# A ninth gate tile in the scan's block, early loads of the first experts, and a last stage by column halves

## What is computed

```python
z = h @ p['w_in']                      # its last 3*1024 columns are the three branch gates zg
# three mixers on parts of z: RWKV-7 time mixing (both directions), 2-D attention, S5 state space
gates = jax.nn.sigmoid(zg).reshape(..., 3, D_MODEL)
merged = jnp.sum(jnp.einsum('btnc,ncd->btnd', y, p['w_branch']) * gates, axis=2)
x = layer_norm(alpha * x + gate1 * (merged @ p['w_out']))
h = x * (1 + scale2) + shift2
# router: the 8 best of 64 experts for each token, with a weight each; 1 shared expert for all
y = sum over the 8 experts of  weight * (silu(h @ w_gate[e]) * (h @ w_up[e])) @ w_down[e]
x = layer_norm(alpha * x + gate2 * (y + y_shared))
```

## Time and profile before

| | us |
|---|---|
| median of 3 runs (lowest, highest) | 2002.49 (1999.87, 2004.68) |
| the profiled execution's own time | 1999.28 |
| its span in the profile | 1997.5 |

### The profile page before, as it was taken

How to read it: one execution, slowest core, us unless ns; L and a number is a source line. 1 busy time by engine, 2 the same in 40 slices (tenths; PEclk the granted TensorE clock), 3 DMA queues, 4 the chain that set the end, 5 groups by cost and what they waited for, 6 DMA issues and landing times. The chain is left out here.

```text
span 1997.5 us, 44977 instructions
## 1 busy us (share of the span) xinstructions
PE 1810.6 (91%) x18164; PEld 1300.7 (65%) x18164; DVE 1014.6 (51%) x2092; ACT 493.1 (25%) x936; POOL 674.5 (34%) x1021
## 2 busy tenths in 40 slices
PE   7989999989788999999999879997699999999967
PEld 2555655455556776777777669545587888778833
DVE  3769865728634555555555467467422222222218
ACT  2111133130033443343443322012122222112200
POOL 5517000000013443444444253221354454444430
PEclk9989999989889999999999989997799999999989
DMA  9133557663233122222210167300799999998956
GB/s 303 53 129 102 181 196 243 209 241 133 74 92 115 53 71 68 75 73 76 73 58 9 42 220 266 126 32 11 281 342 336 329 303 329 342 329 305 362 218 278
DMA packets 228097, 353.30 MB, mean 177 GB/s; under 512 B 38274, under 2 KB 156821, under 8 KB 224485
## 3 DMA queue, kind: packets, MB, share of 16 engines
q1 hardware_dynamic: 201070, 298.11, 43.9%
q0 software_dynamic: 23840, 42.65, 6.0%
q10 hardware_dynamic: 3030, 10.28, 1.4%
HBM read 305.80 MB, written 83.03 MB: 195 GB/s over the span
## 5 line engine op out<-in xcount | busy, mean ns | idle before, releaser
L2922 DVE TENSOR_TENSOR me_hh<-me_sg,ps_ju 128x128 f32<-128x128 f32 x76 | 21.9, 289 | 375.5 <-PE ps_jd L2874 363.8
L460 PE MATMUL ps_s<-hT,w_in_sb 128*128 128x512 f32 x432 | 192.3, 598 | 0.0
L2866 PE MATMUL ps_jg<-me_xT,me_wg 128*128 128x128 f32 x1216 | 152.7, 280 | 4.7 <-DVE me_hh L2922 4.7
L2866 PE MATMUL ps_ju<-me_xT,me_wu 128*128 128x128 f32 x1216 | 149.3, 276 | 0.0
L2866 PEld LDWEIGHTS ps_jg<-me_xT,me_wg 128*128 128x128 f32 x1216 | 146.0, 197 | 5.1 <-issue 5.0
L1356 PE MATMUL ps_gs<-hT,gt_w 128*128 128x512 f32 x256 | 145.9, 653 | 3.2 <-PEq L84 3.2
L2874 PE MATMUL ps_jd<-me_wd,me_hh 128*128 128x512 f32 x304 | 143.1, 593 | 2.4 <-DVE me_yb L2928 2.4
L2866 PEld LDWEIGHTS ps_ju<-me_xT,me_wu 128*128 128x128 f32 x1216 | 143.2, 193 | 0.0
L460 PEld LDWEIGHTS ps_s<-hT,w_in_sb 128*128 128x128 f32 x432 | 80.8, 192 | 91.9 <-issue 91.1
L2895 ACT ACTIVATE me_xT<-ps_jx 128x1024 f32<-128x1024 f32 x77 | 78.9, 1025 | 210.1 <-PE ps_jx L2857 210.1
L2814 POOL TENSOR_TENSOR me_scr<-me_scr 128x1 f32<-128x1 f32 x312 | 66.0, 212 | 186.2 <-DVE me_yb L2928 169.9
(11 more groups left out here) (579 smaller groups left out, 3785.9 us busy)
## 6 DMA issues: line engine op xcount, KB each, us to landing
me_wg<-in_exp_w_gate SPq DMA_DIRECT2D x76, 512.0 KB, 5.5
me_wu<-in_exp_w_up SPq DMA_DIRECT2D x76, 512.0 KB, 7.7
me_wd<-in_exp_w_down SPq DMA_DIRECT2D x76, 512.0 KB, 5.8
w_ad_sb<-in_w_ada SPq DMA_DIRECT2D x32, 512.0 KB, 4.1
w_in_sb<-in_w_in SPq DMA_DIRECT2D x31, 512.0 KB, 4.5
gt_w<-in_w_in SPq DMA_DIRECT2D x24, 512.0 KB, 4.8
cb_rows<-yj_dram SPq DMA_DIRECT2D x5, 2048.0 KB, 21.2
zr<-in_w_ada SPq DMA_DIRECT2D x4, 2048.0 KB, 9.2
```

Of the source, the lines that this page charges most:

```text
L460: mm(ps_s[:, b, :], w_in[:, r, k, :], hT[:, k, 0:TS], start=(k == 0), stop=(k == KT - 1))
L2866: last = mm(o[:, 0:P], w[:, s, k, :], xT[:, s % 2, k, :], start=(k == 0), stop=(k == KT - 1))
```

## The change

It has four parts.

1. GT_S5 becomes 9. The scan's block computes nine gate tiles, the RWKV stage 15. Its pattern is left as it is, so the last 8 G steps are empty.
2. Between the merge and the residual stage the semaphores are cleared as elsewhere, but for three that are still in use, and the semaphores of the expert loads are made there.
3. The weights of the first four jobs are loaded in the residual stage. For this `jobs` is written behind the first token tile's tables, not the last's; SP then loads gate and up weights for jobs 0 to 3 and the down weights of job 0, into a place of their own (`sb_ahead`), and the expert stage starts with the down weights of jobs 1 to 3. The zeros in `me_xg` are written in three pieces ahead of the shared expert's product on GpSimd, as each part of the buffer comes free.
4. In the last stage TensorE takes the first column half of a tile (from the second tile on) through all six rows and then the second; VectorE takes its two additions, the product with gate2, the sum and the statistics by halves. The separate form for the last tile is gone.

```diff
-GT_S5 = 8
+GT_S5 = 9
 # merge_buffers: rooms for the vectors of the last stage and the expert weights, reserved ahead
+        sb_ahead(moe, "hot_room", [P, NT * TOPK * P - 4 * D])
+        m.e_wg, m.e_wu = sb_ahead(moe, "me_wg", [P, JG, KT, E_F]), sb_ahead(moe, "me_wu", [P, JG, KT, E_F])
+        m.e_wd = sb_ahead(moe, "me_wd", [P, JG, D])
...
 # residual stage, SP, behind the stores of h2
+                sp.wait_ge(m.o_mm, NT)
+                sp.wait_ge(m.t_jobs, 1)
+                for s in range(JG):
+                    e = sp.value_load(m.jobs[0:1, s:s + 1], min_val=0, max_val=E_N - 1)
+                    load_up(m, a, sp, s, e)
+                    if s == 0:
+                        load_down(m, a, sp, s, e)
...
 # residual stage, GpSimd
+                pool.wait_ge(m.o_h2, NT)
+                G.memset(m.xg[:, 2:4], 0.0)
+                for b, t in ((1, NT - 2), (0, NT - 1)):
+                    pool.wait_ge(m.o_t_mm, 2 * t + 2)
+                    pool.wait_ge(m.o_hw[b], 16 * ((t + 2) // 2))
+                    G.memset(m.xg[:, b], 0.0)
                 for c, sl in enumerate(halves):
...
                     G.tensor_tensor(hh[:, sl], sg[:, sl], hu[:, sl], ALU.mult).then_inc(m.u_hh, 1)
-                pool.wait_ge(m.o_t_mm, 2 * NT)
-                pool.wait_ge(m.o_hw[0], 16 * ((NT + 1) // 2))
-                pool.wait_ge(m.o_hw[1], 16 * (NT // 2))
-                G.memset(m.xg[:], 0.0)
...
 # residual stage, VectorE
                     last.then_inc(m.t_hot, 1)
-                dve.wait_ge(m.t_row, 1)
-                V.tensor_copy(m.jobs[:], ps_je[0:1, 0:P])
+                    if t == 0:
+                        dve.wait_ge(m.t_row, 1)
+                        V.tensor_copy(m.jobs[:], ps_je[0:1, 0:P]).then_inc(m.t_jobs, 1)
...
 # last stage, TensorE, tiles 1 to 4
+                        for h in range(2):
+                            for j in range(BYPE):
+                                if h == 0:
+                                    landed(j)
+                                last = product(j, h)
                             last.then_inc(m.e_mm, 1)
 # last stage, VectorE, tiles 1 to 4
+                        dve.wait_ge(m.e_land[b % NR], 16 * (b // NR + 1))
+                        for h, sl in enumerate((left, right)):
+                            dve.wait_ge(m.e_mm, 2 * t + 1 + h)
+                            summed = V.scalar_tensor_tensor(tmp[:, sl], first[:, sl], m.gj[:, t, BYPE:BYPE + 1], ps[:, t % 2, sl],
+                                                            ALU.mult, ALU.add)
...
+                            link(V.scalar_tensor_tensor(tmp[:, sl], second[:, sl], m.gj[:, t, BYPE + 1:TOPK], tmp[:, sl], ALU.mult, ALU.add))
+                            link(V.tensor_tensor(tmp[:, sl], tmp[:, sl], g2[:, c, sl], ALU.mult))
+                            link(V.tensor_tensor(x[:, sl], x[:, sl], tmp[:, sl], ALU.add))
+                            link(V.bn_stats(st[:, t, h], x[:, sl]))
...
 # build, behind the merge stage
-                nc.all_engine_barrier()
+                kept = [m.o_w, m.o_x, m.o_g]
+                m.phase_sems = [x for x in m.phase_sems if x not in kept]
+                clear_sems(nc, m)
+                m.phase_sems += kept
```

More of the change, by code:

```diff
@@ L1035, in _ @@
                 for b in range(2):
-                    sp.wait_ge(g5_out[b], 16 * (GT_S5 // 2))
+                    sp.wait_ge(g5_out[b], 16 * len(range(b, GT_S5, 2)))
             @block.tensor
@@ L1346, in sp_lane @@
         for b in range(2):
-            sp.wait_ge(out[b], 16 * ((GT - GT_S5) // 2))
+            sp.wait_ge(out[b], 16 * sum(t % 2 == b for t in range(GT_S5, GT)))
     def pe_lane(pe):
@@ L3037, in _, with product, landed @@
                     pe.wait_ge(m.e_dg, t + 1)
-                    if t >= 2:
-                        pe.wait_ge(m.e_used, 2 * t - 3)
-                    for j in range(BYPE):
+                    if t == 2:
+                        pe.wait_ge(m.e_used, 1)
+                    elif t > 2:
+                        pe.wait_ge(m.e_red, t - 2)
+                    def product(j, h):
+                        return nc.tensor.matmul(ps[:, t % 2, ts512(h)], weight(t)[:, j, :], rows[piece(t, j) % NR][:, j % HALF, ts512(h)],
+                                                start=(j == 0), stop=(j == BYPE - 1))
+                    def landed(j):
                         b = piece(t, j)
@@ L3045, in _ @@
                             pe.wait_ge(m.e_land[b % NR], 16 * (b // NR + 1))
+                    if t == 0:
+                        for j in range(BYPE):
+                            landed(j)
+                            for h in range(2):
+                                last = product(j, h)
+                            if j == HALF - 1 or j == BYPE - 1:
+                                last.then_inc(m.e_mm, 1)
+                    else:
                         for h in range(2):
-                            last = nc.tensor.matmul(ps[:, t % 2, ts512(h)], weight(t)[:, j, :], rows[b % NR][:, j % HALF, ts512(h)],
-                                                    start=(j == 0), stop=(j == BYPE - 1))
-                        if j == HALF - 1 or j == BYPE - 1:
+                            for j in range(BYPE):
+                                if h == 0:
+                                    landed(j)
+                                last = product(j, h)
                             last.then_inc(m.e_mm, 1)
@@ L3087, in _ @@
-                    norm_stats(V, dve, link, m, x, st[:, t], mv[:, t], m.e_sqv, m.e_sq, t)
+                        dve.wait_ge(m.e_used, 1)
+                        V.scalar_tensor_tensor(tmp, second, m.gj[:, t, BYPE + 1:TOPK], tmp, ALU.mult, ALU.add).then_inc(m.e_used, 1)
+                        dve.wait_ge(m.e_used, 2)
+                        link(V.tensor_tensor(tmp, tmp, g2[:, c], ALU.mult))
+                        link(V.tensor_tensor(x, x, tmp, ALU.add))
+                        V.bn_stats(st[:, t, 0], x[:, left])
```

72 lines of the change are left out of this document (44 added, 28 removed).

## The result

| | before | after |
|---|---|---|
| median of the runs beside it (us) | 2004.68 (7 runs, 1997.13 to 2010.34) | 1987.79 (7 runs, 1981.77 to 1993.30) |
| ratio to before, 95% interval | | 0.9923 (0.9897 to 0.9949) |
| the same, timed once more | | 0.9913 (0.9879 to 0.9947) |
| span of the profiled execution | 1997.5 | 1991.8 |
| the same, profiled once more | 1994.6 | 1980.4 |

The change makes the kernel 15.4 us faster by the first ratio and 17.4 by the second (each ratio's interval reaches from 10 to over 20), where 21.7 were forecast. The two profiled executions of the prediction's kernels differ by only 5.7, and a second pair by 14.2: one pair of traces is too coarse to check the sum, so I check it term by term, and take each term as a mean over all the traces that hold the code in question (fourteen in the end, two each of before and after among them).

What follows compares the result with a forecast made beforehand. Each stage has its own limit between barriers, so an edit acts on its stage's last wait. Terms sum to -21.7: 1977.6 from the profiled execution, 1980.8 from the median, middle 1979.2 us; 1973 to 1985 at 0.64, wider 1970 to 1990.

Steps and rivals of the forecast that it cites:

- the tenth unit: Rival: the tenth RWKV unit is a chain of latencies, so removal gives 2.5, not 7.4; 1984 us; chance 0.08.
- the stretched operation: Rival at the residual stage's end: VectorE's 3.59 operation has another cause than GpSimd's zeros; 5.5 less, 1984.7; chance 0.04.
- the lead eaten: Rival in the expert stage: DMA is the limit, later waits grow, 7 of the 11.5 are lost; 1986; chance 0.13.
- scan's block: End of the scan's block: SP waits for the ninth gate tile's store to land; a loss of 2.7 us.
- tenth unit: Tenth RWKV unit: eight weight rows of gate work leave TensorE; a gain of 7.4 us (5 to 8.6).
- seam to the merge: From the tenth unit to the merge: SP waits only for the attention output; a gain of 3.3 us.
- clearing, merge to residual: Between merge and residual stage: more range clears on GpSimd; a loss of 1.0 us (0.5 to 2.7).
- residual stage's end: Residual stage's end: zeros gone from beside VectorE's operation, TensorE's gap shrinks and the clock may hold; a gain of 5.5 us.
- start of the expert stage: Expert stage's start: early loads let gathers and vectors land sooner; a gain of 11.5 us (6 to 14).
- last stage: Last stage: VectorE's work by halves makes a tile about 10.95, above TensorE's 10.3; a loss of 2.3 us.
- Does the lead last?: Expert stage: TensorE sets the pace, busy throughout from 1620 to 1640, so the lead from the start stays.
- The slower case: Rival in the expert stage: every gather lands later; at 0.5 a job the time is 2017; chance 0.03.

Runs made afterwards that it cites:

- half dose: After with the zeros of two of the four row buffers back at the old place, beside VectorE's 40-column operation; executed once, in 2005.79 us.
- the base rows one job later: After with VectorE's scaling of the base rows, which waits for the vectors, moved behind the second job's multiplication instead of the first's; 0.9906 of before.

## Why the prediction was right, and where it was short

The direction was right, and the time of 1987.79 lies inside the range of 1970 to 1990, but outside the band of 1973 to 1985 that had most of the chance. It was the width of the range that held it. The time is nearer to the rivals' 1986, 1984.7 and 1984 than to my 1979.2; the traces clear two of them (the tenth unit, the stretched operation) and leave the first, the lead eaten, open in part. Of the 8.6 between 1979.2 and 1987.79, 3.8 are the kernel before, which ran at 2004.68 beside it where the sum took 2000.9; the other 4.8 are the sum, which promised 21.7. The terms, as the prediction put them, beside the mean of the traces that have the old or the new code at that place:

| term | forecast | measured | means, old to new (traces) |
|---|---|---|---|
| scan's block | +2.7 | +3.0 | 103.27 to 106.24 (3, 9) |
| tenth unit | -7.4 | -8.0 | 54.06 to 46.10 (3, 11) |
| unit seven | none | +1.9 | 53.43 to 55.34 (3, 11); see below |
| seam to the merge | -3.3 | -2.3 | 14.35 to 12.00 (3, 11) |
| clearing, merge to residual | +1.0 | +1.0 | 2.43 to 3.42 (4, 10) |
| residual stage's end | -5.5 | -5.4 | 24.55 to 19.18 (4, 9) |
| start of the expert stage | -11.5 | -8.1 | 43.06 to 35.00 (5, 5) |
| last stage | +2.3 | +2.1 | 51.55 to 53.61 (7, 7) |
| sum | -21.7 | -15.8 | |

**Scan's block**: as forecast. SyncE takes VectorE's place as the last, and with its wait gone the cost goes.

**Tenth unit**: right, and the 1.25 that I took off in all was 0.6 too much. There is no chain of latencies: that rival (1984) fell.

**Seam**: the mechanism held, the size did not. I gave the attention output's store a landing a little shorter than the 3.04 of two gate stores. It was longer: issued at 1140.03, SyncE goes on at 1143.66, 3.63; over the eleven traces 3.08 to 3.67, mean 3.4, where the two gate stores had 3.04 in all three. The step that failed is "one transfer alone should land a little sooner than two", and it is half of the missing 1.0. The other half is a stretch that I left as it was, from there to TensorE's first product: 8.55 (1143.66 to 1152.21) for 8.14, and in the means 8.8 for 8.3. Why it grew is open.

**Clearing**: TensorE's gap between the two stages is 3.42 against 2.43, in every trace. The whole 1.0 stands at the merge's end; the residual stage's end shows none of it (GpSimd starts 1.6 after the table, where it was 2.2).

**Residual stage's end**: right in both parts. The half dose shows that VectorE is held to the end of GpSimd's zeros, and behind the gap of 1.79 the sixteen products take 2.04 at a granted clock of 1.00; at gaps of 3.50 and 5.21 they take 3.75. That the shorter gap keeps the clock held in nine of ten traces; in that of the base rows one job later the sixteen took 3.33 behind a gap of 1.80. The Trainium skill, page "SBUF — State Buffer", section "Who interferes with whom", has the first issuer hold the port, for a VectorE operation that takes the shared pair. In this kernel VectorE started 0.04 to 0.05 ahead of GpSimd in all five traces with zeros there and was the one that waited: here the trace differs, if the start that it shows is the moment of issue, and the rival built on that rule fell.

**Start of the expert stage**: 3.4 short, the largest miss. In the means of five traces each the first `up` came 3.8 sooner for my 5 and the third 6.4 for my 9.6. Two steps of the working failed, both on landings. First, "the first took about the median and I give it 4": with three down loads issued around it, it took 6.25, and 3.38 with them behind it. I had priced the loads left over as if they came beside the gather, but SyncE puts two of them ahead. By itself that was nothing to win: with the loads moved behind, the second gather was late and the first `up` came later still (15.5 for 14.1). Second, the vectors: 12.55 from issue to landing for my 10.5, because I counted the traffic until then (3.5 MB) and the next jobs' loads, issued from 1408.6 on, came on top. Some 4.0 MB moved in that time (12.55 us at 322 GB/s), with the DMA engines nearly full from 1404 on. Before, when the vectors are issued; after, when they are issued; after, the ten us behind that (columns as in the earlier trace rows):

```profile
1414.00:1416.00 2.00, 0.06 (x1) 0.00 (x0) 0.00 (x0) 1.02 (x1) 1.26 (x4) 0.50 1.03 406
```

```profile
1402.00:1404.00 2.00, 2.00 (x12) 1.92 (x11) 0.00 (x0) 1.02 (x1) 1.39 (x5) 0.50 0.32 72
1404.00:1414.00 10.00, 10.00 (x76) 9.41 (x76) 0.29 (x1) 2.60 (x4) 1.02 (x1) 0.92 0.95 350
```

After, the engines are at 0.32 when the vectors are issued, since these stand behind the first rows, and at 0.95 from then on. So bandwidth fits as what the vectors wait for, as the forecast had it; the volume in the sum was too small. Issuing them sooner, into the stretch that has room, was not tried. What is shown is that their wait capped the start: without it the fourth `up` came 3.4 sooner. That the term also missed by 3.4 is chance: this edit takes the whole wait away, and the forecast had only sized it too small.

**Does the lead last?** I said that it does, from windows of before without a gap, as that of 20 us in the earlier trace rows. Windows of 100 us of the same trace, from 1450 to 1850, have TensorE idle for 0.3 to 4.5 us each, so that evidence was weak. From the fourth `up` on, four traces with the late start took 468.9 to 475.4, mean 471.3, and eight with the early one 470.1 to 482.2, mean 475.7. The rival "lead eaten" may thus be true in part: 4.4, with a scatter of 3 to 4 in a single trace, so some 2 in the difference. Added to the sum it gives -11.4; the measured times, -15.4 and -17.4, fit little or none of it better, but each interval reaches down to 10. All fourteen runs of after and the twenty-nine of before beside them are 16.0 apart in the mean (12.7 to 19.3). With the down loads gone the stages are equal, so late landings, the rival's mechanism, are what could do it. How much of the lead is lost with all loads in place stays open. The slower case, a loss at every job, is out: it asked for 0.29 a job, 22 us.

**Last stage**: right; a tile of 10.88 for a forecast of 10.95, and no wait on VectorE. The count of four tiles was a little off: by the timeline of before they take 41.3, not 41.6, and 4 x 10.95 is 43.8. Measured, the four cost 2.5 more, and the first tile, which is still whole, 0.4 less, as VectorE no longer waits behind it.

**Unit seven** has no edit and was not in the sum. In ten of eleven traces with nine tiles TensorE stops in it for 0.8 to 2.5, in none of the three with eight. In the second trace of after:

```profile
932.33 0.27 PE L1736 MATMUL ps_c<-rc_a,rc_b 64*64 64x64 f32 x1 [2.17 <-issue]
```

"issue" means that nothing in the profile released it. The traces with eight tiles have such stops too, at other places; in the second trace of before:

```profile
820.99 0.82 PE L1752 MATMUL ps_c<-rc_a,rc_k 64*128 64x128 f32 x10 [1.63 <-issue]
```

Summed over the stage from 560 us on they are 1.7 to 3.7 with eight tiles (mean 2.5) and 1.6 to 3.8 with nine (mean 2.7): with the ninth tile they stand at another place, and hardly more is lost to them. The eight units without an edit, two to nine, took 445.5 to 448.6 with eight tiles (mean 447.1) and 445.8 to 455.6 with nine (mean 449.8). So the 1.9 of unit seven is what that unit lost, and not shown to be a cost of the ninth tile; what causes the stops stays open.

Of the 5.9 by which the sum of the table fell short, 3.4 are the start, 1.9 unit seven (if it is counted), 1.0 the seam and 0.3 the scan's block; the tenth unit and the last stage gave 0.8 back.

## What to carry to other kernels

When loads are moved out of a crowded start, ask what is issued just ahead of the first transfer that an engine waits for, and which engine's queue stands behind the next landing: here moving three loads behind a gather brought that gather 2.9 sooner and the fourth job nothing, as the next gather was then late, while moving one wait in VectorE's queue by a job brought 3.4. Compare stages by their length, from several traces of each kernel, and ask of a stop that shows up in one unit whether the same stop has left another: two executions of the same kernel differed by 11 us in span, twice the smaller of the differences between the kernels. And splitting an elementwise chain into halves costs its fixed part again for each half (0.6 a tile here), which pays only where its engine waits for the producer longer than that.

## What the runs showed of the hardware

A gap on TensorE of the same length costs the clock in some executions and not in others. Two places of the RWKV stage in the one trace of after, with the same four products behind the same wait:

```profile
1075.31 1.11 PE L1522 MATMUL ps_ax<-ident,at_p 128*128 128x128 f32 x4 [2.97 <-ACT at_p L1604]
...
1114.17 0.66 PE L1522 MATMUL ps_ax<-ident,at_p 128*128 128x128 f32 x4 [2.97 <-ACT at_p L1604]
```

The windows on the two (columns as in the earlier trace rows) have a granted clock of 0.50 (1.2 GHz) and of 1.00 (2.4 GHz):

```profile
1075.30:1076.30 1.00, 0.99 (x5) 0.93 (x5) 0.16 (x1) 0.16 (x1) 0.00 (x0) 0.50 0.00 0
1114.20:1114.80 0.60, 0.60 (x5) 0.49 (x5) 0.16 (x1) 0.12 (x1) 0.28 (x1) 1.00 0.00 0
```

Over the fourteen traces there are 42 such gaps of 2.97: the products behind take 0.65 or 0.66 in 26 and 0.98 to 1.12 in 16. Behind the gap of 3.44, 11 of 14 take 1.11 or 1.12. The sixteen `placed` products behind a gap of 1.79 or 1.80 take 2.03 or 2.04 in nine traces and 3.33 in one; behind the gaps of 3.50 and 5.2 they take 3.6 to 3.75 in all five. Parts of the program come in two lengths accordingly, as the merge stage (102.4 or 104.0 from its first product to the next stage's, with the longer clearing 103.5 or 105.0), and a stage with several such gaps scatters: units two to nine took 445.5 to 448.6 in the three traces of the old code. This, with the expert stage, is why a single pair of traces misled.
